# The first norm and the first projection panel of a three-layer block: input tiles loaded first, and the panel's first step issued tile by tile

## The reference

```python
def rmsnorm(x, g):
    x32 = x.astype(jnp.float32)
    y = x32 * lax.rsqrt(jnp.mean(x32 * x32, axis=-1, keepdims=True) + EPS)
    return y.astype(x.dtype) * g
...
    for i in range(DEPTH):
        u = rmsnorm(h, norm_pre[i])
...
    proj = h @ w_in                    # first layer: 1024 x 10240
    qkv = proj[..., :n_qkv].reshape(B, S, 3, N_DIL_GROUPS * DIL_HEADS, HEAD_DIM)
```

## Time and profile before

| what | value |
|---|---|
| median of 3 runs | 2288.2 us (2287.73 to 2288.29) |
| the profiled execution's own time | 2279.71 us |
| its span, first to last instruction | 2277.9 us |
| TensorE busy | 2125.5 us, 93% of the span |
| VectorE, ScalarE, GpSimd busy | 42%, 39%, 37% |
| mean granted TensorE clock | 0.975 |

### The profile page before, as it was taken

One profiled execution on the slowest core, in us unless ns is written; L12 is line 12 of the kernel. 1 busy time (PEld: TensorE's weight loads), 2 busy tenths in 40 slices (PEclk: granted clock), 3 DMA queues, 4 the chain that ended last, 5 costly groups with the idle time before them and its releaser, 6 DMA issues. The chain is left out here.

```text
span 2277.9 us, 26489 instructions
## 1 busy us (share of the span) xinstructions
PE 2125.5 (93%) x10240; PEld 1695.0 (74%) x10240; DVE 947.1 (42%) x1627; ACT 877.5 (39%) x1800; POOL 836.9 (37%) x446
## 2 busy tenths in 40 slices
PE   4999999999969998989999999999989999999998
PEld 3877888878748776668678878876776568888886
DVE  1344444635364365753250641256664633210111
ACT  2554545655454564543231232332332232321221
POOL 2432323333334422253344445333243242444442
PEclk9999999999979999999999999998999999999999
DMA  4322222322342311132352334232243331322321
GB/s 157 93 74 75 70 80 74 94 93 75 94 174 85 98 56 56 56 111 93 94 162 93 97 85 119 79 85 88 79 135 122 132 129 58 100 93 93 102 98 60
DMA packets 129483, 217.07 MB, mean 95 GB/s; under 512 B 8632, under 2 KB 58344, under 8 KB 129152
## 3 DMA queue, kind: packets, MB, share of 16 engines
q1 hardware_dynamic: 110720, 168.63, 24.4%
q0 software_dynamic: 7952, 28.40, 3.7%
q10 hardware_dynamic: 10688, 18.35, 2.3%
HBM read 197.24 MB, written 17.52 MB: 94 GB/s over the span
## 5 line engine op out<-in xcount | busy, mean ns | idle before, releaser
L2455 POOL TENSOR_TENSOR lo_ring<-raw_ring,hi_ring 128x1024 fp32r<-128x1024 f32 (+1 forms) x288 | 690.3, 2421 | 1011.5 <-ACT hi_ring L2103 1011.4
L1047 PE MATMUL bank<-xh,hi_ring 128*128 128x512 f32 (+1 forms) x1536 | 604.9, 394 | 5.5 <-POOL lo_ring L2455 2.8
L1047 PE MATMUL bank<-xh,lo_ring 128*128 128x512 f32 (+1 forms) x1536 | 588.3, 383 | 0.0
L1047 PE MATMUL bank<-xl,hi_ring 128*128 128x512 f32 (+1 forms) x1536 | 587.6, 383 | 0.0
L2103 ACT CAST hi_ring<-raw_ring 128x1024 fp32r<-128x1024 f32 (+1 forms) x288 | 287.8, 1046 | 411.3 <-PE bank L1047 391.4
L1047 PEld LDWEIGHTS bank<-xh,hi_ring 128*128 128x128 f32 x1536 | 290.8, 189 | 74.9 <-issue 19.0
L1047 PEld LDWEIGHTS bank<-xh,lo_ring 128*128 128x128 f32 x1536 | 290.6, 189 | 57.6
L1047 PEld LDWEIGHTS bank<-xl,hi_ring 128*128 128x128 f32 x1536 | 291.0, 189 | 54.1 <-issue 2.6
L1047 PE MATMUL bank<-hi_ring,xh 128*128 128x512 f32 (+1 forms) x512 | 212.8, 416 | 18.7 <-POOL lo_ring L2455 5.8
L1047 PE MATMUL bank<-lo_ring,xh 128*128 128x512 f32 (+1 forms) x512 | 205.6, 402 | 0.0
L1047 PE MATMUL bank<-hi_ring,xl 128*128 128x512 f32 (+1 forms) x512 | 205.4, 401 | 0.0
(11 more groups left out here) (281 smaller groups left out, 2657.9 us busy)
## 6 DMA issues: line engine op xcount, KB each, us to landing
raw_ring<-in_ffn_w_in SPq DMA_DIRECT2D x176, 256.0 KB, 3.1
raw_ring<-in_dil_w_in SPq DMA_DIRECT2D x80, 512.0 KB, 3.7
raw_ring<-in_ffn_w_out SPq DMA_DIRECT2D x44, 512.0 KB, 3.8
raw_ring<-in_diff_w_in SPq DMA_DIRECT2D x32, 512.0 KB, 3.8
raw_ring<-in_w_in SPq DMA_DIRECT2D x32, 512.0 KB, 3.7
arena<-scratch_heads POOLq DMA_DIRECT2D x4, 1584.0 KB, 13.8
scratch_gates<-arena ACTq DMA_DIRECT2D x24, 256.0 KB, 2.1
arena<-scratch_gates POOLq DMA_DIRECT2D x24, 256.0 KB, 4.3
```

The source lines that it names most:

```text
L1047: ins = T.matmul(bank[pb][:, cols if p.form == "feature" else slice(0, p.cols)], lhsT, rhs, start=(k == 0 and m == 0 and half != 1), stop= ...
L2455: G.tensor_tensor(lo, raw_ring[:, p % RAW, 0:q.kq * q.n], hi.bitcast(F32), ALU.subtract).then_inc(lowered, 1)
```

## The change

`norm_to_parts` and the barrier `over` go. `norm_input` writes the start out by hand, and the first panel's generator is begun in it and handed on to `dilated_layer`, which finishes it.

- Each tile of `x` has its own semaphore. ScalarE issues tiles 0 and 2, SyncE issues the 128 columns of `ident`, then tiles 1 and 3, then four weight pieces, then the rest of `consts` and `params`, then the other pieces.
- TensorE waits at first for `ident` alone; every engine waits for the rest of the constants at the new job `settled`, behind the panel's first step.
- GpSimd issues the gain row's load first of all. ScalarE runs a small activation to load its table.
- ScalarE squares all four tiles in a row, rounds two weight pieces, and then follows the tiles. GpSimd lowers pieces 0 and 1 behind the four powers.
- The four `mac` jobs of the panel's first step stand between the norm's tiles, each waiting for its own tile's `lower` alone.

```diff
+    needs = [(), (), (), ()]
+    main = plan.panel("v", "dil_w_in", 6 * D, 512, "tile", at=(0,), look_at=(3, 0), needs=needs)
+    def lower(n):
+        plan.job("lower", n, 4 + 2 * (n % 2))
+        needs[n] = plan.parts[n]
+    for n in range(NT):
+        plan.job("norm_square", n, None)
+    plan.job("norm_scale", 0)
+    plan.job("round_to", 2)
+    tile(0)
+    plan.job("norm_scale", 1)
+    tile(1)
+    plan.job("norm_scale", 2)
+    lower(0)
+    plan.job("norm_scale", 3)
+    plan.job("lower_to", 2)
+    tile(2)
+    next(main)
+    lower(1)
+    plan.job("round_to", 3)
+    tile(3)
+    next(main)
+    lower(2)
+    plan.job("round_to", 4)
+    plan.job("lower_to", 4)
+    next(main)
+    lower(3)
+    next(main)
+    plan.job("settled")
+    return main
...
     plan.job("begin")
-    norm_to_parts(plan, lambda n: None)
-    plan.job("over", False)
-    dilated_layer(plan)
+    dilated_layer(plan, norm_input(plan))
...
         def sync_program(SP):
-            SP.dma_start(consts[:, :], I["consts"]).then_inc(consts_landed, 16)
-            SP.dma_start(params[:, :], I["params"]).then_inc(consts_landed, 16)
+            SP.dma_start(consts[:, 0:P], I["consts"][:, 0:P]).then_inc(ident_landed, 16)
+            for n in (1, 3):
+                SP.dma_start(x[:, n, :], I["x"][n * P:(n + 1) * P, :]).then_inc(x_landed[n], 16)
             for p, q in enumerate(pieces):
+                if p == RAW:
+                    SP.dma_start(consts[:, P:], I["consts"][:, P:]).then_inc(consts_landed, 16)
+                    SP.dma_start(params[:, :], I["params"]).then_inc(consts_landed, 16)
...
# ScalarE
                 if kind == "begin":
-                    for n in range(NT):
-                        A.dma_start(x[:, n, :], I["x"][n * P:(n + 1) * P, :]).then_inc(x_landed, 16)
-                    A.wait_ge(consts_landed, 32)
-                    A.wait_ge(x_landed, 16 * NT)
+                    for n in (0, 2):
+                        A.dma_start(x[:, n, :], I["x"][n * P:(n + 1) * P, :]).then_inc(x_landed[n], 16)
+                    A.wait_ge(halves_set, 1)
+                    A.activation(square_tmp[:, 0:36], minus_half[:, :], ACT.Square).then_inc(table_loaded, 1)
+                    A.wait_ge(table_loaded, 1)
+                elif kind == "round_to":
+                    splits(a[0])
...
# GpSimd
                 if kind == "begin":
+                    load_row("pre0", gain_row[:, :], gain_landed)
                     G.memset(minus_half[:, :], -0.5).then_inc(halves_set, 1)
                     G.wait_ge(halves_set, 1)
+                elif kind == "lower_to":
+                    splits(a[0])
+                elif kind == "settled":
                     G.wait_ge(consts_landed, 32)
-                    G.wait_ge(x_landed, 16 * NT)
-                    load_row("pre0", gain_row[:, :], gain_landed)
```

More of the change, by code:

```diff
@@ L215, in run_all, with norm_input, tile @@
         pass
[L218 to L225, removed]
+def norm_input(plan):
+    needs = [(), (), (), ()]
+    main = plan.panel("v", "dil_w_in", 6 * D, 512, "tile", at=(0,), look_at=(3, 0), needs=needs)
+    def tile(n):
+        plan.tile_parts("norm_tile", n)
+    def lower(n):
[26 more added lines that the diff above has]
+    return main
 BY_TILE = [(m, b) for b in range(4) for m in range(2)]
@@ L334, in projections @@
         c = g * D + hf * 512
-        if g < 2:
+        if u == 0:
+            yield from begun
+        elif g < 2:
             yield from plan.panel("v", w, 6 * D + c, 512, "group" if g else "tile", at=(u,))
@@ L800, in program @@
         rounded, lowered, stepped = sem("piece_rounded"), sem("piece_lowered"), sem("stepped")
-        consts_landed, x_landed, halves_set = sem("consts_landed"), sem("x_landed"), sem("halves_set")
+        ident_landed, consts_landed, halves_set = sem("ident_landed"), sem("consts_landed"), sem("halves_set")
+        table_loaded = sem("table_loaded")
+        x_landed = [sem(f"x_landed{n}") for n in range(NT)]
         gain_landed, row_landed = sem("gain_landed"), sem("row_landed")
-        over = {name: sem(f"over_{name}") for name in ("pe", "dve", "act", "pool")}
         v_step, a_step = sem("v_step"), sem("a_step")
@@ L1342, in tensor_program @@
                 if kind == "begin":
-                    begin()
+                    T.wait_ge(ident_landed, 16)
+                elif kind == "settled":
+                    T.wait_ge(consts_landed, 32)
                 elif kind == "mac":
                     mac(*a)
[L1346 to L1350, removed]
                 elif kind == "norm_tile":
@@ L2091, in scalar_program, with splits @@
             ys = Tally()
-            def splits(s):
-                while seen.n < min(steps[s].ahead, len(pieces)):
+            def splits(limit):
+                while seen.n < min(limit, len(pieces)):
                     p = seen.n
@@ L2361, in scalar_program @@
                 elif kind == "mem_kv":
-                    splits(a[0])
+                    splits(steps[a[0]].ahead)
                 elif kind == "mem_keep":
```

22 lines of the change are left out of this document (6 added, 16 removed).

## The result

| | before | with the change |
|---|---|---|
| median, first set of runs | 2288.24 us (4 runs, 2287.73 to 2291.16) | 2267.89 us (4 runs, 2266.98 to 2272.13) |
| the same kernels again | 2288.46 us (11 runs, 2283.95 to 2293.11) | 2270.89 us (6 runs, 2266.43 to 2273.42) |
| ratio | | 0.9912, 95% interval 0.9895 to 0.9929; again 0.9921, 0.9905 to 0.9937 |

The forecast was 2269.6 us in a range of 2265 to 2276; both medians lie inside it. The change takes off some 18 to 20 us, 0.8 to 0.9%. The medians of one kernel move by up to 3 us between the sets, so no more than that can be read from a single median.

What follows compares the result with a forecast made beforehand. Loads and norm ran serially at the start, delaying TensorE's weight matmuls. The profiled execution's 2279.71 less 18.6 us gives 2261.1; with the median's unchanged distance of 8.5 us the forecast is 2269.6 us, range 2265 to 2276.

Steps and rivals of the forecast that it cites:

- What bounds the start: Kernel start: loads and norm do not overlap; overlapping them starts weight matmuls 21.0 us earlier, for a gain of 18.6 us.
- Landing times from bytes: Loads at the start: x tiles land at 5.9, 8.5 and 9.8 us, weight pieces 0 and 1 at 11.1 and 12.5.
- ScalarE's order: ScalarE at the start: squares until 12.1 us, two weight pieces rounded until 14.1, then casts of tile 0 until 15.3.
- GpSimd: GpSimd at the start: fourth power takes 1.54 us, until 18.0; pieces 0 and 1 then lowered at 20.4 and 22.7.
- The port: VectorE's two-input scaling of tile 3 beside GpSimd's lowering: piece 1 delayed 0.4 us, between nothing and 0.75.
- The clock: TensorE's first step: first 12 matmuls at the lowered clock, 0.427 us apart; step ends at 36.1 instead of 54.90.
- Rival 1: First weight matmuls: clock already up and a landing 0.5 us faster; gain 20.6, 2267.6 us; chance 0.14.
- The transposes: TensorE: eight transposes take 1.97 us at granted 1.0 and 0.5 alike, so say nothing of the clock they ran at.
- Rival 3: First step: transposes hold the clock down, so token tile 1's 12 matmuls cost 2.4 us more; 2272.0 us; chance 0.08.
- The distance of 8.5 us: Whole kernel: runs' median stands 8.5 us above the profiled execution; taken as unchanged and added to 2261.1.
- Rivals 4 and 5: Behind the first step: gain lost to new waits (2280 partial, 2288 full; 0.05), or slower, 2293 or more (0.01).
- rival 5: Later stages: shifted starts create about ten more lowered-clock stretches of 2.4 us each; 2293 us or more; chance 0.01.

Runs made afterwards that it cites:

- e11: Changed kernel with the gain row loaded on ScalarE's queue between x tiles 0 and 2, no longer by GpSimd; median 2272.72 us (4 runs).
- e9: Changed kernel with VectorE scaling tile 3 only when GpSimd has lowered weight piece 1; median 2269.09 us (4 runs).
- e3: Changed kernel with the rest of consts and params issued right behind ident, ahead of x tiles 1 and 3 and the weights; median 2275.27 us, ratio 0.9947.
- e7: Changed kernel with unread transposes of the identity where TensorE is idle: 36 ahead of tile 0, 30 behind tile 1, 8 behind tile 2; median 2269.22 us.
- e1: Changed kernel with the old job order and barrier put back, so only the new loads and early table load stay; median 2277.96 us, ratio 0.9955.
- e4: Kernel before the change, run again without edit for a second trace; median 2288.61 us (12 runs).
- e2: Changed kernel with the first step's four mac jobs behind all four tiles of the norm; median 2270.61 us (6 runs).
- e5: Changed kernel with the mean and power of tile 3 moved ahead of the lower of tile 0; median 2269.18 us (4 runs).
- e12: Changed kernel run again without edit, for a second trace and more times; median 2270.89 us (6 runs).

## Why the prediction was right

- **What bounds the start.** Right: the mark moved by 20.8 us in the first trace (19.7 to 20.0 in the second, against the two of before), and the medians by 20.4 and 17.6. The gain went into the sum as 18.6, so that the forecast lies within 2 us of either median is in part the noise of the medians.
- **Landing times from bytes.** Forecast 5.9, 8.5 and 9.8 us for x, 11.1 and 12.5 for pieces 0 and 1; ScalarE's rows show work released at 4.76, 7.98 (tile 1), 11.95 and 13.31. Right to 1.2 us. Unseen: the gain row landed at 9.6, not 5.9, and kept VectorE idle for 3.61 us. It cost nothing that the mark shows: e11, without that wait, has it 0.35 later.
- **ScalarE's order.** Right: the casts of tile 0 at 14.1 forecast, 14.26 found.
- **GpSimd.** Right: pieces from 18.0 forecast, 17.79 found; the fourth power took 1.52 beside VectorE, 1.54 forecast.
- **The port.** I took 0.4 us for piece 1 between a bound of nothing and 0.75. It was 1.0 (3.35 against 2.35), outside my upper bound, since the longest lowering of the whole trace before was 3.09. The Trainium skill's rule ("SBUF — State Buffer", on the shared port pair), an exclusive lock for the whole instruction, gave 1.28 and was nearer. e9 agrees with it from both sides: with VectorE held back piece 1 took 2.37 us, and the scaling that then met piece 2 took 3.28 instead of 1.28.
- **The clock.** This is the term that was mis-sized. I took 12 matmuls at 0.427 and the transposes of tile 3 at the lower level. In the first trace six matmuls ran so, and nine in the second (12 in e3). The other six of the first trace took 1.5 us instead of 2.6, and the transposes with their start 0.8 instead of 2.1; against these 2.4 us stands piece 1, 0.4 later than forecast. So the step ended at 34.07 and not at 36.1, and the mark moved by 20.8 and not by 18.6. (Of the 18.8 that the forecast's own end gives, 0.2 were taken off as rounding, with no row behind it.) Rival 1's gain of 20.6 came out in the first trace, but not by its condition: the clock was not up when the weight matmuls started, it rose after six of them.
- **The transposes.** My reading of the earlier trace rows failed, that eight transposes take 1.97 us at a granted 1.0 and at a granted 0.5 alike and say nothing of the clock. They take 1.03 to 1.09 at the higher level. So the clock of before was at the lower level already while its four groups of transposes ran, at 1.94 or 1.97 us each, and not only after the 5.2 us of idle time that rival 1 counts on. The 1.00 that the stretches show near the start can't be trusted; it looks like what is printed ahead of the first recorded change. In the trace of the change the stretch from 20 to 23.3 us reads 1.00 while its matmuls are 0.43 apart:

```profile
20.00:23.30 3.30, 2.90 (x6) 1.82 (x6) 2.42 (x3) 1.00 (x2) 3.30 (x2) 1.00 0.54 162
```

Rival 3 fell in both traces of the change: token tile 1's matmuls ran at the higher level. The Trainium skill ("TensorE: Matmul & The Clock Gate", on transposes) holds that transpose mode does not count for the clock gate. e7 measures otherwise for these fp32 transposes.
- **The distance of 8.5 us** between the profiled execution and the median of before I took as unchanged. It was a property of that one execution. The sum held because adding 8.5 back brought it to the median of before less the gain; taken off the profiled time alone, the gain would have given 2261.1, below every run of the change.
- **Rivals 4 and 5.** Nothing was given back by waits, as the waits behind the mark and the table show. The clock in later stages does move the time by several us from execution to execution, in both kernels: before ran from 2281.3 to 2292.8 over the 18 runs beside e1 to e4. A part of the gain, 3.3 us at the mean, may have gone there; that is rival 5's mechanism at a small size, and it stays open.

## What to carry to other kernels

When a start is two serial halves, transfers and then compute, look first at the order of the loads and at preparing the weights under the norm: here they brought 10.9 and some 5 us; slicing the first step finely (e2) brought 1 us at most. Look for the job in whose shadow a slow engine starts: one tiny mean behind a bulky operation held GpSimd for 3 us. Then ask who follows: with it moved, TensorE started 0.65 us earlier only (e5). And when a gain is smaller than 1%, compare marks at fixed places of the traces and many runs of each kernel with the clock's cost taken off, never two profiled spans.

## What the runs showed of the hardware

- Eight 128x128 fp32 transposes take 1.97 us at the lower clock and 1.03 to 1.09 at the higher, and a run of transposes alone raises it (e7; in e12 the norm's own do).
- A VectorE operation with two SBUF inputs and GpSimd's subtraction take turns: 1.28 becomes 2.69 (change) or 3.28 us (e9) on VectorE, 2.35 becomes 3.35 on GpSimd (change).
- Executions of the same kernel differ by up to 0.5% (2281.3 to 2292.8 us), and in the two traces of before the difference lies where TensorE is granted 0.5 in one and 1.0 in the other.
- A 512 KB row broadcast issued first on GpSimd's queue landed 8.3 us after its issue in the change, beside the x tiles and weights on the two other queues; the x tiles landed after 5.6 (ScalarE's queue) and 7.6 us (SyncE's) at the median. Before, issued at 15.77 us with the others nearly done, the same row took 4.5 us.
